# The first norm's sum of squares in a two-block transformer kernel: fewer sums on TensorE, more adds on GpSimd

## The reference, cut to what matters

```python
def rms_norm(x, g):
    xf = x.astype(jnp.float32)
    y = xf * lax.rsqrt(jnp.mean(xf * xf, axis=-1, keepdims=True) + EPS)
    return (y * g.astype(jnp.float32)).astype(x.dtype)

def diff_attn_layer(h, g_norm, w_qkv, ...):
    xn = rms_norm(h, g_norm)
    qkv = xn @ w_qkv
    ...
```

## Time and profile before

| | |
|---|---|
| median of 3 runs | 1229.19 us (1228.75 to 1229.86) |
| the profiled execution | 1229.36 us, span 1227.6 us |
| TensorE busy | 1218.4 us, 99% of the span |
| VectorE, ScalarE, GpSimd busy | 887.1, 704.3 and 160.5 us |
| the four sums over the features (line 1216) | from 18.31 us on, behind step 2 |
| mean granted clock of TensorE | 0.998 of full |

### The profile page before, as it was taken

The page is one execution under the profiler, slowest core; times in us unless marked ns, Lnnn a source line. Parts: engine busy times, 40 slices in busy tenths (PEclk is TensorE's granted clock), DMA queues, the critical chain, the costliest instruction groups (busy, mean ns, idle before and its releaser), DMA issues.

```text
span 1227.6 us, 26433 instructions
## 1 busy us (share of the span) xinstructions
PE 1218.4 (99%) x10067; PEld 1178.2 (96%) x10067; DVE 887.1 (72%) x1744; ACT 704.3 (57%) x1402; POOL 160.5 (13%) x166
## 2 busy tenths in 40 slices
PE   8999999999999999999999999999999999999998
PEld 8998999999997799999999899999999999999998
DVE  6988777776778977777678977766565877676543
ACT  6878555554465746555448865554345775555432
POOL 1111400002301040000562013000120002200000
PEclk9999999999999999999999999999999999999999
DMA  8333454534543135444467335555553333555551
GB/s 339 124 118 107 156 174 175 181 136 168 203 153 114 50 139 201 171 175 148 178 221 261 116 138 194 184 188 189 187 190 140 138 138 138 195 183 188 190 183 58
DMA packets 31711, 203.45 MB, mean 166 GB/s; under 512 B 3632, under 2 KB 4656, under 8 KB 11264
## 3 DMA queue, kind: packets, MB, share of 16 engines
q1 hardware_dynamic: 30672, 198.67, 45.1%
q0 software_dynamic: 800, 3.21, 0.7%
q10 hardware_dynamic: 144, 0.28, 0.1%
HBM read 201.09 MB, written 1.05 MB: 165 GB/s over the span
## 4 chain that ended last, share of the span: by engine, by line
PE 92%; DVE 5%; ACT 1%; issue 1%; DMA 0%; SPq 0%; DVEq 0%; ACTq 0%
PE ps L746 27%; PE ps L747 27%; PE ps L748 27%; DVE w_lo L1876 1%; PE ps L1166 1%; PE ps L1132 1%; PE ps L841 1%; PE ps L1151 1%; PE ps L842 1%; PE ps L843 1%; PE ps L967 1%; PE ps L971 1%; PE ps L1008 1%; DVE E_S L2340 1%; PE ps L988 0%
## 5 line engine op out<-in xcount | busy, mean ns | idle before, releaser
L1876 DVE TENSOR_TENSOR w_lo<-raw,w_hi 128x1024 fp32r<-128x1024 f32 (+2 forms) x392 | 463.1, 1214 | 88.8 <-ACT w_hi L1367 87.9
L1367 ACT ACTIVATE w_hi<-raw 128x1024 fp32r<-128x1024 f32 (+2 forms) x392 | 377.1, 1002 | 184.4 <-PE ps L748 184.1
L746 PE MATMUL ps<-x_hi,w_hi 128*128 128x256 f32 (+2 forms) x1384 | 397.6, 287 | 2.5 <-issue 1.8
L747 PE MATMUL ps<-x_lo,w_hi 128*128 128x256 f32 (+2 forms) x1384 | 392.8, 284 | 0.0
L748 PE MATMUL ps<-x_hi,w_lo 128*128 128x256 f32 (+2 forms) x1384 | 392.3, 283 | 0.0
L746 PEld LDWEIGHTS ps<-x_hi,w_hi 128*128 128x128 f32 x1384 | 261.3, 189 | 4.6 <-issue 2.5
L747 PEld LDWEIGHTS ps<-x_lo,w_hi 128*128 128x128 f32 x1384 | 260.9, 189 | 0.5
L748 PEld LDWEIGHTS ps<-x_hi,w_lo 128*128 128x128 f32 x1384 | 261.0, 189 | 0.0
L746 PE MATMUL ps<-X_x_hi,w_hi 128*128 128x256 f32 (+2 forms) x568 | 162.5, 286 | 0.0
L748 PE MATMUL ps<-X_x_hi,w_lo 128*128 128x256 f32 (+2 forms) x568 | 161.2, 284 | 0.0
L747 PE MATMUL ps<-X_x_lo,w_hi 128*128 128x256 f32 (+2 forms) x568 | 160.8, 283 | 0.0
(11 more groups left out here) (352 smaller groups left out, 1846.9 us busy)
## 6 DMA issues: line engine op xcount, KB each, us to landing
raw<-in_weights SPq DMA_DIRECT2D x159, 1024.0 KB, 4.8
raw<-in_weights SPq DMA_DIRECT2D x32, 704.0 KB, 4.0
raw<-in_weights SPq DMA_DIRECT2D x4, 832.0 KB, 4.5
E_bias<-in_even_bias POOLq DMA_DIRECT2D x4, 768.0 KB, 9.4
raw<-in_weights SPq DMA_DIRECT2D x4, 512.0 KB, 7.6
out<-h SPq DMA_DIRECT2D x8, 128.0 KB, 5.1
cst<-in_consts SPq DMA_DIRECT2D x1, 808.0 KB, 12.5
h<-in_tokens SPq DMA_DIRECT2D x1, 544.0 KB, 6.4
```

The costliest lines, as they stand in the source:

```text
L746: pe.matmul(target, hi, xs[0], start=start, stop=False)
L747: pe.matmul(target, hi, xs[1], start=False, stop=False)
L1367: act.activation(w_hi[:, to + a:to + b], raw[:, fr + a:fr + b], ACT.Copy).then_inc(hi_made, 1)
L1876: dve.tensor_tensor(w_lo[:, to + a:to + b], raw[:, fr + a:fr + b], w_hi[:, to + a:to + b].bitcast(F32), ALU.subtract).then_inc(lo_made, 1)
```

## The change

GpSimd adds further: after the two adds it had, it adds chunks 2 and 3 onto 0 and 1 (544 columns), waits for that, and adds chunk 1 onto chunk 0 (272 columns). TensorE waits for the fourth add in place of the first two, and multiplies one chunk by the ones instead of four.

```diff
             def first_sums():
-                for c in range(4):
-                    pe.wait_ge(first_added, c // 2 + 1)
-                    mm = pe.matmul(bank(4, 0, T), ones[:, :], oA["sq"][:, c * T:c * T + T], start=c == 0, stop=c == 3)
-                mm.then_inc(summed, 1)
+                pe.wait_ge(first_added, 4)
+                pe.matmul(bank(4, 0, T), ones[:, :], oA["sq"][:, 0:T], start=True, stop=True).then_inc(summed, 1)
...
                 pool.wait_ge(first_sq, 4 + 4 * i)
                 to = oA["sq"][:, 2 * i * T:2 * (i + 1) * T]
                 pool.tensor_tensor(to, to, oA["sq"][:, (2 * i + 4) * T:(2 * i + 6) * T], ALU.add).then_inc(first_added, 1)
+            for i, n in enumerate((2 * T, T)):
+                pool.wait_ge(first_added, 2 + i)
+                pool.tensor_tensor(oA["sq"][:, 0:n], oA["sq"][:, 0:n], oA["sq"][:, n:2 * n], ALU.add).then_inc(first_added, 1)
```

## The result

The changed kernel takes 1232.41 us, the median, where the kernel before takes 1229.19: a ratio of 1.0024 (the two medians themselves divide to 1.0026), 95% interval 1.0015 to 1.0033. The profiled execution took 1232.41 us with a span of 1230.6, against 1229.36 and 1227.6. It is slower by 3.2 us; 1232.6 was forecast.

What follows compares the result with a forecast made beforehand. TensorE, busy 99% of the span, was taken to bound the kernel. A shift of +1.9 us from its wait, less sums saved, plus +1.5 for the clock made +3.4: 1229.19 to 1232.6 us, range 1230.8 to 1234.2.

Steps and rivals of the forecast that it cites:

- What goes, 1.38 us: TensorE's sums: of eight multiplications' records, 1.84 us in all, one multiplication of 0.46 us stays, so 1.38 us goes.
- The turns of GpSimd and VectorE: GpSimd's new adds and VectorE's splits of slot 2 take turns, so the fourth add ends only at 21.53 us.
- The wait, 3.3 us and +1.9: TensorE idles before the sum from 18.31 to 21.61 us; less the sums saved, everything behind shifts by +1.9 us.
- The clock, +1.5: TensorE's granted clock falls to half during the wait or at its end, for 3.4 us, costing +1.5 us.
- rival B: TensorE's wait comes but the clock does not fall: +1.9 us, 1231.1; chance 0.17.
- rival E: Clock low for a second stretch, or VectorE's late work catches TensorE in steps 4 to 6: +1.5 more, 1234.1; chance 0.10.
- Everything else, at nothing: Ln, `rstd`, VectorE's tables, the late second split and TensorE's later waits move along with the delay, costing nothing more.
- rival D: TensorE's later waits on VectorE in this layer absorb part of the shift: -0.5 to -1.6, 1231.0 to 1232.1; chance 0.07.
- Rival C: Slot 2's splits come at another time, GpSimd's adds are not held up: shift 0, 1229.2, up to 1230.7; chance 0.09.

Runs made afterwards that it cites:

- Experiment 1: The changed kernel, but TensorE waits only for the second add and sums one ready chunk, both new adds kept: 1228.33 us, ratio 0.9989.
- Experiment 2: The changed kernel with VectorE splitting slot 2 only behind GpSimd's fourth add: 1229.3 us, ratio 1.0.
- experiment 10: The changed kernel with 16 useless matmuls ahead of TensorE's wait for the adds: 1231.07 us, ratio 1.0014.
- experiment 7: The changed kernel with slot 2's splits behind the fourth add and the one sum inside step 3, behind its fourth chunk: 1228.66 us, ratio 0.9993.
- experiment 11: Experiment 7 again with no edit: 1229.14 us, ratio 0.9997.
- Experiment 8: The kernel before, four sums and no further adds, with sums, Ln, Exp and the turn of `rstd` one step later: 1231.11 us, ratio 1.0013.
- experiment 6: The changed kernel without the fourth add; TensorE waits for the third and sums two chunks: 1229.34 us, ratio 0.9999.
- experiment 4: The changed kernel with its one sum, Ln, Exp and the turn of `rstd` one step later: 1230.62 us, ratio 1.0012.
- experiment 3: The changed kernel with 24 useless matmuls ahead of TensorE's wait for the adds: 1231.13 us, ratio 1.0013.

## Why the prediction was right

The time was 1232.4, the forecast 1232.6, and the case was the forecast's own: a wait of TensorE and a clock fall behind it. By its steps:

- **What goes, 1.38 us.** Experiment 1 takes the sums and not the wait, and gives 1.3.
- **The turns of GpSimd and VectorE.** Foretold for the third add, second split and fourth add: about 2.3, 2.3 and 1.6 us. The rows have 2.19, 2.35 and 1.62. The third add is shorter because the first split began a little earlier against it (16.94 and 17.28, where 17.37 and 17.5 were taken). Experiment 2 takes the splits away and gets the lengths of the adds alone.
- **The wait, 3.3 us and +1.9.** It was 3.21 and +1.83 in the profile; experiment 10, with the clock held up, gives +1.7 in the medians. TensorE was idle from 18.02 to 21.23, where 18.3 to 21.6 was said; both ends moved with the start-up.
- **The clock, +1.5.** It was +1.55 in the profile, 3.4 us at half as was said. The size was right, and the account of it incomplete: it was priced as one fall each time. By the mean clock it falls in two runs of three (the range of the changed kernel is 1230.6 to 1234.5, that of the kernel before beside it 1228.7 to 1230.6), and sometimes stays twice as long. The median falls among the runs with one fall, so the likeliest case gave the median. That it came within 0.2 us is in part luck: the mix of runs decides where the median lies, and in the second timing it lay at 1232.78. The ground on which the fall was forecast was also thinner than it looked. The prediction argued from the pause near the start, 1.8 us with a fall behind it. The profiles of experiments 7, 10 and 11 have pauses of 1.1 to 1.3 us there and no fall, that of experiment 2 has one of 1.0 and a fall. Rivals B and E, at 0.17 and 0.10, are both in the scatter of one kernel.
- **Everything else, at nothing.** Right for this change: the distance at 120 us is that of the span, and the later waits are the same (0.24 and 0.25 us in the rows above), so rival D's absorption did not happen. It was right only because all of TensorE's queue moved by the same 3 us. Experiment 8 shows what a late `rstd` does when TensorE does not wait as well: 1.7 us. That the argument "what they wait for moves along" has this condition was not in the prediction.
- **Rival C.** Its mechanism is real and was right in its price: with the splits elsewhere the change costs nothing (1229.3 against 1229.62), and gains nothing either.

What stays open is what sends the clock down in one run and not in the next, for once or twice 3.4 us, when the kernel is the same. No run without a fall was profiled, so that its wait was as long, too, is not shown. The two timings of the changed kernel show that it varies, not by what.

## What to carry to other kernels

Before moving work from the engine that bounds a kernel onto an idle one, take the time at which the bounding engine will want the result and the time at which it is ready, and count in which instructions of other engines it takes turns with: here the cover was 0.92 us, the adds alone took 2.1 and beside VectorE's splits 3.8, for 1.38 us saved. A pause put into a busy TensorE can cost its length and a stretch of half clock again; here shortening the pause from 3.2 to 1.3 us, even by useless matmuls, took the second price away. A reduction that ends late can be moved to a later place in the queue, but whoever takes its result further, here VectorE's rotary tables, has to be followed to its own next deadline first.

## What the hardware showed that was not expected

- **The length of a pause and the clock.** Behind single pauses of an otherwise busy TensorE of 0.94, 1.13, 1.31, 1.36 and 1.45 us (experiments 2, 10, 6, 8 and 4) the granted clock stayed at full, 2.4 GHz; at the end of the 3.05 us pause it fell to 1.2 GHz in both profiles of the changed kernel, for 3.4 us in one and 6.8 in the other. The length of one pause doesn't decide by itself, though. Near the start of experiment 2 TensorE paused for 1.04 and 0.86 us, and the clock fell:

```profile
7.11 0.36 PE L746 MATMUL ps<-x_hi,w_hi 128*128 128x272 f32 x1 [1.04 <-issue]
8.99 0.39 PE L746 MATMUL ps<-x_hi,w_hi 128*128 128x272 f32 x1 [0.86 <-DVE x_lo L1944]
...
9.50:12.80 3.30, 3.30 (x15) 3.02 (x14) 2.98 (x6) 3.30 (x8) 0.00 (x0) 0.50 1.05 421
```

  In experiment 10 it did not fall behind the one at the start:

```profile
7.38 0.56 PE L746 MATMUL ps<-x_hi,w_hi 128*128 128x272 f32 x1 [1.32 <-issue]
```

- **The half clock at the start comes and goes between runs.** It lies at 8.1 to 11.5 us in the kernel before, begins at 7.3 in both profiles of the changed kernel and at about 9.5 in those of experiments 2 and 3, and is absent in those of experiments 7, 10 and 11. This is a stretch of experiment 10, where the earlier trace rows have 0.50:

```profile
7.20:10.60 3.40, 3.22 (x13) 3.12 (x14) 2.93 (x8) 2.77 (x7) 0.00 (x0) 1.00 1.03 415
```

  Its price is small and not settled. TensorE is done with step 2 at 18.68 us there, and at 18.31 and 18.02 in kernels where the clock had fallen; but where it fell latest, in experiments 2 and 3, TensorE is done latest too, at 19.15 and 19.29. And of the 91 runs of the kernel before, the 21 with a mean clock of 1.0 have a median of 1229.04 us and the 34 with 0.998 one of 1229.72. Behind 21 us, where TensorE waits for nobody, the same fall costs 1.5 to 1.8 us.
- **Who goes first hangs on some 0.2 us.** In experiment 3 the third add was issued 0.08 us ahead of the split and took 1.37; in experiment 10 its record begins 0.16 behind the split's and it took 2.28, in the changed kernel 0.34 behind and 2.19.
